# Hidden tiles turned by DMA from the first step on, and dilated scores as three single-pass products, in a two-layer transformer trunk

## The reference

```python
D_FF = ((8 * D_MODEL + 3 * 256 - 1) // (3 * 256)) * 256      # 2816
DIL_PATTERNS = ((128, 1), (512, 4), (2048, 16))

def dilated_mixer(a, cos, sin, w_in, w_o):
    proj = (a @ w_in).reshape(B, S, N_DIL, 3, H, DH)
    for gi, (window, dil) in enumerate(DIL_PATTERNS):
        q = partial_rope(proj[:, :, gi, 0], cos, sin)
        k = partial_rope(proj[:, :, gi, 1], cos, sin)
        v = proj[:, :, gi, 2]
        o, lse = banded_attention(to_residue(q, dil)[:, :, :, None], to_residue(k, dil),
                                  to_residue(v, dil), window // dil)
    ...
    alpha = jax.nn.softmax(jnp.stack(lses, axis=-1), axis=-1)
    o = jnp.einsum('bshn,bshnd->bshd', alpha.astype(a.dtype), jnp.stack(outs, axis=3))
    return o.reshape(B, S, H * DH) @ w_o

def swiglu(h, w_gu, w_down):
    gu = h @ w_gu
    g, u = gu[..., :D_FF], gu[..., D_FF:]
    return (jax.nn.silu(g) * u) @ w_down

def reference(x, positions, ...):
    h = x
    for i in range(DEPTH):                       # DEPTH = 2: layer 0 NSA, layer 1 dilated
        a = rmsnorm(h, norm_mix_pre[i])
        m = nsa_mixer(a, ...) if i % 2 == 0 else dilated_mixer(a, ...)
        h = h + rmsnorm(m, norm_mix_post[i])
        f = swiglu(rmsnorm(h, norm_ffn_pre[i]), ffn_w_gu[i], ffn_w_down[i])
        h = h + rmsnorm(f, norm_ffn_post[i])
    return h
```

## Time and profile before

| | |
|---|---|
| median of the runs | 814.19 us |
| the profiled execution, its own time | 814.93 us |
| its span, first to last instruction | 812.9 us |
| TensorE busy | 801.4 us |
| VectorE busy | 511.5 us |
| ScalarE busy | 455.5 us |
| GpSimd busy | 96.7 us |
| granted TensorE clock (mean) | 0.998 |

### The profile page before, as it was taken

The page is one execution under the profiler, slowest core; times in us unless marked ns, Lnnn a source line. Parts: engine busy times, 40 slices in busy tenths (PEclk is TensorE's granted clock), DMA queues, the critical chain, the costliest instruction groups (busy, mean ns, idle before and its releaser), DMA issues.

```text
span 812.9 us, 11748 instructions
## 1 busy us (share of the span) xinstructions
PE 801.4 (99%) x4377; PEld 643.5 (79%) x4377; DVE 511.5 (63%) x1073; ACT 455.5 (56%) x879; POOL 96.7 (12%) x159
## 2 busy tenths in 40 slices
PE   9999999999999999999999999999999999999996
PEld 7877675788888888788877878878877888888885
DVE  5966979786646464686565665666568765555444
ACT  7836878764535353575555666555558553535331
POOL 1000005700222222000000000000000012222210
PEclk9999999999999999999999999999999999999999
DMA  9955211166986687558444535363434667767711
GB/s 318 346 186 197 88 54 53 63 223 195 234 216 191 191 244 216 170 194 273 153 160 145 167 115 197 104 206 105 156 110 142 196 226 203 207 184 238 224 32 52
DMA packets 126312, 141.69 MB, mean 174 GB/s; under 512 B 23680, under 2 KB 109744, under 8 KB 126128
## 3 DMA queue, kind: packets, MB, share of 16 engines
q1 hardware_dynamic: 125168, 136.73, 54.6%
q0 software_dynamic: 992, 4.19, 1.3%
q10 hardware_dynamic: 96, 0.02, 0.0%
HBM read 134.64 MB, written 2.10 MB: 168 GB/s over the span
## 4 chain that ended last, share of the span: by engine, by line
PE 83%; DMA 6%; issue 4%; POOL 3%; DVE 2%; ACT 1%; POOLq 0%; ACTq 0%; DVEq 0%
PE ps L1785 73%; PE ps L1794 6%; DMA planes_t<-planes 6%; POOL ht L684 2%; PE ps L2062 2%; PE ps L2035 2%; POOL planes L679 1%; PE ps L1847 1%; PE ps L2073 1%; ACT junk L740 0%; ACT xd_hi L728 0%; DVE w_lo L1231 0%; DVE h L1555 0%; DVE h L1561 0%; DVE tmp L1559 0%
## 5 line engine op out<-in xcount | busy, mean ns | idle before, releaser
L1231 DVE TENSOR_TENSOR w_lo<-w_raw,w_hi 128x1024 fp32r<-128x1024 f32 x240 | 288.5, 1229 | 73.3 <-ACT w_hi L719 71.0
L719 ACT ACTIVATE w_hi<-w_raw 128x1024 fp32r<-128x1024 f32 x240 | 246.1, 1061 | 2.9 <-DMA w_raw<-in_ffn_w_gu 2.7
L1785 PE MATMUL ps<-w_hi,xt_hi 128*128 128x512 f32 x472 | 188.8, 401 | 0.0
L1785 PE MATMUL ps<-w_hi,xt_lo 128*128 128x512 f32 x472 | 183.6, 390 | 0.0
L1785 PE MATMUL ps<-w_lo,xt_hi 128*128 128x512 f32 x472 | 183.0, 390 | 0.0
L1785 PE MATMUL ps<-w_hi,xd_hi 128*128 128x512 f32 x288 | 117.4, 408 | 0.2 <-DVE w_lo L1231 0.2
L1785 PE MATMUL ps<-w_hi,xd_lo 128*128 128x512 f32 x288 | 113.2, 393 | 0.0
L1785 PE MATMUL ps<-w_lo,xd_hi 128*128 128x512 f32 x288 | 112.8, 392 | 0.0
L1785 PEld LDWEIGHTS ps<-w_hi,xt_hi 128*128 128x128 f32 x472 | 88.5, 188 | 24.5 <-issue 8.2
L986 ACT ACTIVATE silu<-ps,rs 128x256 f32<-128x256 f32 x44 | 20.9, 474 | 151.2 <-PE ps L1785 151.1
L1785 PEld LDWEIGHTS ps<-w_hi,xt_lo 128*128 128x128 f32 x472 | 88.6, 188 | 18.8
(11 more groups left out here) (259 smaller groups left out, 936.0 us busy)
## 6 DMA issues: line engine op xcount, KB each, us to landing
w_raw<-in_ffn_w_gu SPq DMA_DIRECT2D x88, 512.0 KB, 5.1
w_raw<-in_dil_w_in SPq DMA_DIRECT2D x72, 512.0 KB, 4.6
w_raw<-in_ffn_w_down SPq DMA_DIRECT2D x44, 512.0 KB, 4.9
w_raw<-in_nsa_w_in SPq DMA_DIRECT2D x20, 512.0 KB, 7.3
w_raw<-in_nsa_w_o SPq DMA_DIRECT2D x8, 512.0 KB, 4.7
w_raw<-in_dil_w_o SPq DMA_DIRECT2D x8, 512.0 KB, 4.4
w_k<-in_nsa_cmp_wk SPq DMA_DIRECT2D x2, 1024.0 KB, 9.1
w_raw<-in_nsa_cmp_wv SPq DMA_DIRECT2D x2, 1024.0 KB, 11.6
```

What stands on the lines that cost most here:

```text
L719: act.activation(w_hi[:, n.slot, c:c + 1024], w_raw[:, n.slot, c:c + 1024], ACT.Copy)\
L1231: dve.tensor_tensor(w_lo[:, n.slot, c:c + 1024], w_raw[:, n.slot, c:c + 1024], w_hi[:, n.slot, c:c + 1024].bitcast(F32), ALU.subtract)\
L1785: ins = pe.matmul(o, s, m, start=start, stop=stop, **kw)
```

## The change

Three things.

1. `XBAR` now also holds the tiles (0,0), (1,0) and (1,1). They go over GpSimd and the DMA transpose, and their three `ht_turn` of each layer leave TensorE's list. GpSimd parts (0,0) before it issues the gain load of the network, and merges it after. VectorE and ScalarE take piece n0+6 ahead of `ht_out(1,0)`.
2. In the last step `ht_out(9,1)` stands behind `silu_step(10,0)` and `hs_step(10,0)` on both engines.
3. In the dilated layer the dilation-one scores are three single-pass products for each head, after the 64 x 64 blocks. ScalarE's turned copy of these tiles is `qk_hi`; VectorE writes the rest (`qk_lo`, `dil_turn_lo`, six instructions for each of eight tiles). The patterns are projected in the order 1, 2, 0 (group 0) or 1, 0, 2. Since `qk_lo` lies partly on the gain's buffer, the gain of layer 1's mixer is loaded after the last scores, no longer after the last projection.

```diff
@@ -80,9 +80,14 @@
+def qk_order(g):
+
+    return (1, 2, 0) if g == 0 else (1, 0, 2)
+
...
-XBAR = range(2, FJ - 1)
+XBAR = [(0, 0), (1, 0), (1, 1)] + [(j, m) for j in range(2, FJ - 1) for m in range(MT)]
...
@@ -477,11 +497,9 @@
             def turns_before(n):
 
                 for layer, first in enumerate((N_FFN0, N_FFN1)):
-                    for j in XBAR:
-                        if n == first + 3 * j + 6:
-                            turn_planes(layer, j, 0)
-                        if n == first + 3 * j + 8:
-                            turn_planes(layer, j, 1)
+                    for j, m in XBAR:
+                        if n == first + max(3 * j + 6 + 2 * m, RING):
+                            turn_planes(layer, j, m)
 
...
@@ -670,21 +688,30 @@
 
                 return t.bitcast(U16).rearrange("p (i k) -> p k i", k=2)
 
+            def split_hidden(layer, j, m):
+
+                pool.wait_ge(hs_ready, ffn_order(layer, j, m) + 1)
+                pool.tensor_copy(view(planes, (j % 2 * MT + m) * 512, [[256, 2], [1, 256]]), halves_of(hs[:, m, :]))\
+                    .then_inc(planes_ready, 1)
+
+            def merge_hidden(layer, j, m):
+
+                pool.wait_ge(planes_turned[m], 16 * xbar_of(layer, j, m))
+                if (j - 2, m) in XBAR:
+                    pool.wait_ge(ht_ready, ffn_order(layer, j - 2, m) + 1)
+                pool.tensor_copy(halves_of(ht[:, j % 2, m, :]),
+                                 view(planes_t, (j % 2 * MT + m) * 512, [[256, 2], [1, 256]])).then_inc(ht_merged, 1)
+
             def turn_hidden(layer):
 
-                for j in XBAR:
-                    for m in range(MT):
-                        at = (j % 2 * MT + m) * 512
-                        pool.wait_ge(hs_ready, ffn_order(layer, j, m) + 1)
-                        pool.tensor_copy(view(planes, at, [[256, 2], [1, 256]]), halves_of(hs[:, m, :]))\
-                            .then_inc(planes_ready, 1)
-                        pool.wait_ge(planes_turned[m], 8 * (xbar_no(layer, j, 0) + 2))
-                        if j - 2 >= XBAR[0]:
-                            pool.wait_ge(ht_ready, ffn_order(layer, j - 2, m) + 1)
-                        pool.tensor_copy(halves_of(ht[:, j % 2, m, :]), view(planes_t, at, [[256, 2], [1, 256]]))\
-                            .then_inc(ht_merged, 1)
+                merge_hidden(layer, *XBAR[0])
+                for j, m in XBAR[1:]:
+                    split_hidden(layer, j, m)
+                    merge_hidden(layer, j, m)
 
             for b in range(1, 4):
+                if b != 2:
+                    split_hidden(b // 2, *XBAR[0])
                 pool.wait_ge(h_ready[b][1], MT)
                 if b != 2:
                     post_gain(b + 1, *nexts[b])
@@ -697,7 +724,7 @@
                     pool.wait_ge(sq_h[2], MT)
                     pool.dma_start(h[:, :, :], h_rows.rearrange("(p m) c -> p m c", m=MT)).then_inc(h_permuted, 16)
 
-                    pool.wait_ge(proj_done[1], LAST_E)
+                    pool.wait_ge(scores[1], 8 * DIL_G)
                     post_gain(b + 1, *nexts[b])
                 if b != 2:
...
@@ -1032,10 +1057,10 @@
                         step(it * 2 + (2 + s), Piece(n0 + 8 + 6 * it + 3 * s))
                 j, nx = FJ - 1, Piece(n0 + 3 * FJ - 1)
                 split(nx)
-                ht_out(j - 1, 1)
                 split(nx + 1, (0,))
                 silu_step(j, 0)
                 split(nx + 1, (1,))
+                ht_out(j - 1, 1)
                 ht_out(j, 0)
                 split(nx + 2, (0,))
                 post_squares(b + 1, 0)
...
@@ -1670,12 +1696,31 @@
                 dve.tensor_tensor(x16, rope_a[:, :, :], rope_b[:, :, :], ALU.add).then_inc(roped[1], 1)
                 dve.wait_ge(roped[1], x.qk_no + 1)
 
+            def dil_turn_lo(x):
+
+                if x.kind != QK or x.pat:
+                    return
+                dve.wait_ge(turn_out[1], x.qk_no + 1)
+                at = qk_slot(x.g, 0) * 4 * S
+                src = (2 + x.qk_no % 2) * 512
+                for hp in range(2):
+                    for par in range(2):
+                        to, dims = 32 * x.m + P * par, [[64, 2], [1, 32]]
+                        dve.scalar_tensor_tensor(view(qk_lo[hp], to, dims), view(ps, src + P * hp + par, [[2, 2], [4, 32]]),
+                                                 -SCALE, view(qk_hi, at + hp * S + to, dims).bitcast(F32),
+                                                 ALU.mult, ALU.subtract)
+                for hp in range(2):
+                    to, dims = x.m * 64, [[P, 2], [1, 64]]
+                    ins = dve.tensor_tensor(view(qk_lo[2 + hp], to, dims), view(ps, src + (2 + hp) * P, [[1, 2], [2, 64]]),
+                                            view(qk_hi, at + (2 + hp) * S + to, dims).bitcast(F32), ALU.subtract)
+                ins.then_inc(qk_lo_ready, 1)
+
             def dil_mask(g, t):
                 for w in pair_units(g, t):
                     dve.wait_ge(scores[1], w + 1)
...
@@ -1736,6 +1781,7 @@
                     split(n + k, (0,))
                 dil_attend(2 * e, True)
                 dil_attend(2 * e + 1, False)
+                dil_turn_lo(TILES[e - 1])
                 if e > 4:
                     split(n + k, (1,))
                 dil_attend(2 * e + 1, True)
@@ -2292,7 +2338,7 @@
                     gu(j, 0, pc)
                     down(j - 1, 0, pc + 2)
                     pe.wait_ge(hs_ready, ffn_order(layer, j - 1, 1) + 1)
-                    gu(j, 1, pc, mid=(lambda: ht_turn(1, 1)) if j == 2 else None)
+                    gu(j, 1, pc)
                     down(j - 1, 1, pc + 2)
 
                 def need(m):
@@ -2306,11 +2352,10 @@
 
                 gu(0, 0, Piece(n0), need=need(0))
                 gu(1, 0, Piece(n0 + 2), mid=turn_h)
-                pe.wait_ge(xt_ready[b], 3)
-                ht_turn(0, 0)
+                pe.wait_ge(hs_ready, ffn_order(layer, 0, 0) + 1)
                 gu(0, 1, Piece(n0), need=need(1))
                 down(0, 0, Piece(n0 + 4), first=True)
-                ht_turn(1, 0)
+                pe.wait_ge(hs_ready, ffn_order(layer, 1, 0) + 1)
                 gu(1, 1, Piece(n0 + 2), mid=lambda: ht_turn(0, 1))
                 down(0, 1, Piece(n0 + 4), first=True)
                 assert owed[0] == 0
...
@@ -2376,30 +2423,43 @@
 
                 return view(qk_t, (qk_slot(g, pat) * 4 + 2 * t + j // 2) * S + c, [[step, n]],
                             p0=DH * (j % 2), n=DH)
+
+            def first_hi(g, t, j, c, n):
+
+                return view(qk_hi, (qk_slot(g, 0) * 4 + 2 * t + j // 2) * S + c, [[1, n]], p0=DH * (j % 2), n=DH)
+
+            def first_lo(t, j, c, n):
+
+                return view(qk_lo[2 * t + j // 2], c, [[1, n]], p0=DH * (j % 2), n=DH)
 
             def dil_scores(g, t):
                 (m, hp), ws = dil_unit(t), pair_units(g, t)
                 if ws[0] >= 2:
                     pe.wait_ge(masked[1], ws[0])
-                for odd, w in enumerate(ws):
-                    j = 2 * hp + odd
-                    mm(bank(score_bank(w), 0, S), head(g, 0, 0, j, m * P, P), head(g, 0, 1, j, 0, S), True, True)
+                if t == 0:
+                    pe.wait_ge(qk_lo_ready, 2 * (g + 1))
+                js = (2 * hp, 2 * hp + 1)
                 for pat in (1, 2):
                     for cls in range(2):
                         for odd, w in enumerate(ws):
                             j, c = 2 * hp + odd, cls if pat == 1 else 1 - cls
-                            ins = mm(ps[64 * cls:64 * cls + 64, score_bank(w), 256 + c:DIL_N:2],
+                            mm(ps[64 * cls:64 * cls + 64, score_bank(w), 256 + c:DIL_N:2],
                                      head(g, pat, 0, j, m * P + 64 * cls, 64), head(g, pat, 1, j, m * P + c, 64, 2),
-                                     True, True)
-                            if pat == 2 and cls:
-                                ins.then_inc(scores[1], 1)
+                               True, True)
+                for j, w in zip(js, ws):
+                    mm(bank(score_bank(w), 0, S), first_hi(g, 0, j, m * P, P), first_hi(g, 1, j, 0, S), True, False)
+                for j, w in zip(js, ws):
+                    mm(bank(score_bank(w), 0, S), first_hi(g, 0, j, m * P, P), first_lo(1, j, 0, S), False, False)
+                for j, w in zip(js, ws):
+                    mm(bank(score_bank(w), 0, S), first_lo(0, j, m * P, P), first_hi(g, 1, j, 0, S), False, True)\
+                        .then_inc(scores[1], 1)
 
             def dil_turn_probs(w):
                 pe.wait_ge(normed[1], w + 1)
                 if w >= 1:
                     pe.wait_ge(pt_out[1], w)
                 for k in range(3):
-                    ins = turn(PT_BANK, k, probs[:, w % 4, P * k:P * k + P])
+                    ins = turn(PT_BANK, k, probs_dil[w % 4][:, P * k:P * k + P])
                 ins.then_inc(pt_psum[1], 1)
 
```

(39 more changed lines are left out.)

20 lines of the change are left out of this document (11 added, 9 removed).

## The result

| | before | after |
|---|---|---|
| median of 6 runs each | 814.36 us | 818.99 us (817.76 to 819.84) |
| ratio after/before | | 1.0052, 95% interval 1.0039 to 1.0065 |
| profiled execution, its span | 814.93, 812.9 us | 819.84, 817.6 us |
| mean granted clock | 0.998 | 0.995 |

The change makes the kernel slower by 4.2 us (the ratio times the 814.36 of before). The forecast was 812.9, the range ended at 815.6, and slower had 0.16. The prediction was wrong.

A forecast was written before the change was run, and what follows sets the result against it. TensorE's list was taken to bound the kernel (busy 801 of 812.9 us). Terms -1.5 (turns), -1.04 (last step), -1.3 (scores), +2.5 (waits) give -1.3: from 814.19 to 812.9 us, range 810.8 to 815.6.

The forecast's parts named there:

- What is late is the weight piece, queued on VectorE behind a tile that used to be ready.: At down(0,0), layer 0: TensorE waits 0.47 us for piece n0+4, before any slowing by the gain load.
- The waits are 1.7 and 0.8: 2.5 us lost.: TensorE's waits before down(0,0) in layers 0 and 1, with the transpose slowed 1.2 us by the gain load.
- the middle of two bounds: Delay of tile (0,0)'s transpose by the gain load: between nothing and 2.5 us, taken as 1.2.
- the upper end of the waits: Both waits before down(0,0) together, at the upper bound of the gain load's delay: 5.1 us.
- (1,0) should come under 1 us before down(0,1) asks.: Tile (1,0) reaches st_lo in time and costs nothing; without that cover, up to 0.8 us lost per layer.
- The third rival: Tile (1,0) arrives late and holds ht_out(0,1) on ScalarE and VectorE: 0.8 us per layer, 814.5 us; chance 0.15.
- Six turns, 1.5 us.: Three insertions of turns leave TensorE's list in each of two layers, 0.25 us each: 1.5 us gained.
- Part 2, 1.04: Last step of layer 0: the 1.61 us wait before the turn of (10,0) goes, 0.57 returns; 1.04 us gained.
- part 3, 1.3: Dilated layer's scores: three single-pass products take 0.55 us instead of 0.63, 0.08 a pair, 16 pairs; 1.3 us gained.
- `end_lo` comes 0.57 late: Last step of layer 0: end_lo of (10,0) is ready at 328.25, TensorE asks at 327.73; 0.57 us comes back.
- VectorE's extra work and the gain of the mixer: Dilated layer: 11 us more on VectorE hidden in idle time, mixer's gain load hidden by 1 us; both counted 0.
- The rival on the slower side: Score pairs: single-pass products on half the rows do not overlap, 4.5 us lost instead of 1.3 gained; 818.7 us, chance 0.10.

The follow-up runs named there:

- piece_first: The changed kernel, with VectorE making both halves of piece n0+4's low part before st_lo of tile (0,0) and hs(1,0); 813.37 us, ratio 0.9978.
- filled: The changed kernel with ten more 512-column products on TensorE between gu(0,1) and down(0,0) in both layers, result unread; 816.03 us, ratio 1.0016.
- gain_first: The changed kernel, with GpSimd issuing the gain's load before it parts tile (0,0), not after; 814.22 us, ratio 0.9991.
- first_on_pe: The changed kernel with tile (0,0) turned by TensorE again, which also moved the gain's load behind parting of (1,0); 819.55 us, ratio 1.0053.
- in_time: The changed kernel with gain before parting, piece n0+4 then hs(1,0) before st_lo(0,0), silu(1,0) before st_hi(0,0), (1,0)'s transpose one load earlier; 810.80 us, ratio 0.9944.
- parts23: The changed kernel with tiles (0,0), (1,0) and (1,1) turned by TensorE again, last-step and score changes kept; 812.13 us, ratio 0.9968.
- late_transpose: in_time, but SyncE issues the transpose of (1,0) where the changed kernel does, behind the load of piece n0+8; 812.03 us, ratio 0.9960.

## Why the prediction was wrong, by its own steps

- *What is late is the weight piece, queued on VectorE behind a tile that used to be ready.* Right, in place and cause: `piece_first` takes the wait away without making the tile sooner than it is there.
- *The waits are 1.7 and 0.8: 2.5 us lost.* The step that failed in size: 2.87 and 2.32, 5.2 in all. Of the difference some 0.6 in layer 0 and 0.8 in layer 1 is the way from parting to merge, with the gain's transfer in it. That was taken as 1.2, the middle of two bounds; taking it away saved 1.6 in layer 0 (the merge at 4.43 after parting against 2.83) and 2.2 in layer 1 (4.69 against 2.50), within the bounds of 0 and 2.5. Another 0.4 is the piece and GpSimd's parting beside each other, 2.76 against 2.35, for which the prediction had the row of the piece alone. The rest, 0.2 and 0.3, are handings over.
- The prediction had 5.1 at the upper end of the waits. The measured 5.2 lies just above it (2.87 inside the bound of layer 0, 2.32 above the 2.1 of layer 1). The 5.1 alone gives 812.9 + 2.6 = 815.5, the edge of the range.
- The second step that failed is a cost put at nothing without a reason: after each of these two waits TensorE's clock falls. 3.2 us by the trace, 3.0 by `filled`. `filled` shows the time with the waits as they were and the clock kept: 816.0, or 815.7 by its ratio. So the waits alone bring the time to the edge of the range, 815.6, and the clock carries it 3 us beyond.
- The terms close: 5.2 of waits and 3.2 of clock lost, 1.5, 0.94 and 1.3 gained, is 4.65 us lost in all, and the spans differ by 4.7.
- *(1,0) should come under 1 us before down(0,1) asks.* Right only in the changed kernel, for the reason given there (the stall at down(0,0) gives it time). The cover was thin: with the first wait smaller or gone, the tile cost 0.77 (`gain_first`) and 1.78 us (`piece_first`) in layer 0, 0.35 and 0.53 in layer 1, and more with the gain issued later (`first_on_pe`). The third rival priced it at 0.8 in each layer.
- *Six turns, 1.5 us.* Right: 1.54 in `in_time` against `parts23`.
- *Part 2, 1.04; part 3, 1.3.* Right: 0.94, and 1.3 to 1.4. `end_lo` comes 0.57 late, as written; but the prediction's terms for it add to 328.14, not 328.25, and 328.25 is 0.52 behind 327.73, so that the agreement to the hundredth is chance. A pair's products take 0.55. VectorE's extra work and the gain of the mixer cost nothing that TensorE shows.
- The rival on the slower side (products on half the rows one after the other) was the wrong one: 0.12 a step for two heads, side by side.

What stays open: how the 1.78 at down(0,1) in `piece_first` divides. `late_transpose`, with the gain and hs(1,0) first, still has 0.86 of it, which SyncE's place takes away; the other 0.9 goes with those two, not parted. Why layer 1 shows less of each such wait is open too. That the piece and the parting slow each other is read from rows: both are longer wherever they run side by side, and neither is in `piece_first`, where they do not.
